# A decoder layer on one core: input sums of the seven-product scheme built by accumulating transfers from GpSimd

## The reference

```python
mod = silu(c) @ w_ada + b_ada                 # six shift/scale/gate vectors
h = rms_norm(x) * (1 + scale1) + shift1
proj = h @ w_in                               # columns for two head groups
# group A: 4 heads of gated linear attention; group B: 4 heads of HGRN2
x = x + gate1 * (concat(o_gla, o_hgrn) @ w_out)
h = rms_norm(x) * (1 + scale2) + shift2
x = x + gate2 * (square(relu(h @ w_mlp1)) @ w_mlp2)
return rms_norm(x, final_norm_g)
```

## Time and profile before

| | us |
|---|---|
| median of 3 runs | 1165.91 (1165.58 to 1169.56) |
| the profiled execution | 1166.44 |
| its span, first to last instruction | 1164.7 |
| PE busy in it | 1137.4 |
| DVE busy | 876.3 |
| ACT busy | 612.9 |
| POOL busy | 499.4 |

### The profile page before, as it was taken

How to read it: one execution, slowest core, us unless ns; L and a number is a source line. 1 busy time by engine, 2 the same in 40 slices (tenths; PEclk the granted TensorE clock), 3 DMA queues, 4 the chain that set the end, 5 groups by cost and what they waited for, 6 DMA issues and landing times.

```text
span 1164.7 us, 15675 instructions
## 1 busy us (share of the span) xinstructions
PE 1137.4 (98%) x5555; PEld 939.3 (81%) x5555; DVE 876.3 (75%) x1048; ACT 612.9 (53%) x933; POOL 499.4 (43%) x318
## 2 busy tenths in 40 slices
PE   7999999899999999999999999999999999999996
PEld 6788788787878787888888888888888888788885
DVE  6898888877777677477976765677795884966776
ACT  7763564756566566345654555455664433424424
POOL 1021111534243344427534353344466675666741
PEclk9999999999999999999999999999999999999999
DMA  9777353044353549421455344544624637447203
GB/s 359 259 235 271 128 175 97 1 127 129 93 177 98 154 123 295 143 93 73 137 170 181 136 155 135 181 144 157 194 64 159 223 91 264 147 132 279 72 1 145
DMA packets 160549, 180.44 MB, mean 155 GB/s; under 512 B 7508, under 2 KB 119256, under 8 KB 157784
## 3 DMA queue, kind: packets, MB, share of 16 engines
q1 hardware_dynamic: 160472, 179.44, 46.4%
HBM read 138.51 MB, written 40.89 MB: 154 GB/s over the span
## 4 chain that ended last, share of the span: by engine, by line
PE 89%; DVE 4%; DMA 2%; ACT 2%; issue 1%; SPq 1%; POOL 1%; DVEq 0%; ACTq 0%
PE unit_bank L1742 16%; PE unit_bank L2156 9%; PE unit_bank L2158 9%; PE unit_bank L2157 9%; PE small_bank L2156 9%; PE small_bank L2158 9%; PE small_bank L2157 9%; PE unit_bank L2003 3%; PE small_bank L1742 3%; PE unit_bank L2005 3%; PE unit_bank L2004 3%; PE small_bank L1879 2%; DVE ada_acc L2257 1%; PE small_bank L1781 1%; DMA ada_slot<-in_w_ada_dram 1%
## 5 line engine op out<-in xcount | busy, mean ns | idle before, releaser
L997 POOL TENSOR_TENSOR wr_lo<-quarter,wr_hi 128x512 fp32r<-128x512 f32 x122 | 197.6, 1632 | 174.4 <-ACT wr_hi L1530 174.3
L2156 PE MATMUL unit_bank<-op_hi,wr_hi 128*128 128x512 f32 x452 | 176.5, 390 | 1.1 <-issue 1.1
L2158 PE MATMUL unit_bank<-op_hi,wr_lo 128*128 128x512 f32 x452 | 175.9, 389 | 0.0
L2157 PE MATMUL unit_bank<-op_lo,wr_hi 128*128 128x512 f32 x452 | 175.9, 389 | 0.0
L2156 PE MATMUL small_bank<-op_hi,wr_hi 128*128 128x512 f32 x448 | 174.5, 390 | 0.0
L2158 PE MATMUL small_bank<-op_hi,wr_lo 128*128 128x512 f32 x448 | 174.3, 389 | 0.0
L2157 PE MATMUL small_bank<-op_lo,wr_hi 128*128 128x512 f32 x448 | 174.3, 389 | 0.0
L1530 ACT ACTIVATE wr_hi<-wr_full 128x512 fp32r<-128x512 f32 x90 | 56.8, 631 | 173.3 <-DVE wr_full L2903 173.3
L2903 DVE TENSOR_TENSOR wr_full<-quarter,quarter 128x512 f32<-128x512 f32 x90 | 88.9, 989 | 56.3 <-PE small_bank L2158 23.0
L1530 ACT ACTIVATE wr_hi<-quarter 128x512 fp32r<-128x512 f32 x136 | 83.0, 626 | 90.5 <-PE unit_bank L2158 48.4
L1742 PE MATMUL unit_bank<-a_hi,w_hi 128*128 128x512 f32 x304 | 121.2, 399 | 0.8 <-DVE w_lo L2401 0.8
(11 more groups left out here) (366 smaller groups left out, 2397.2 us busy)
## 6 DMA issues: line engine op xcount, KB each, us to landing
quarter<-in_w_mlp_dram SPq DMA_DIRECT2D x128, 256.0 KB, 4.1
hidden_scratch<-hid SPq DMA_DIRECT2D x98, 256.0 KB, 2.4
ada_slot<-in_w_ada_dram SPq DMA_DIRECT2D x48, 512.0 KB, 6.1
op_full<-hidden_scratch SPq DMA_DIRECT2D x21, 1024.0 KB, 4.8
pair_quarter<-in_w_in_dram SPq DMA_DIRECT2D x32, 256.0 KB, 3.7
piece_x<-t_scratch SPq DMA_DIRECT2D x16, 512.0 KB, 4.1
piece_y<-t_scratch SPq DMA_DIRECT2D x32, 256.0 KB, 3.3
raw<-in_w_out_dram SPq DMA_DIRECT2D x16, 512.0 KB, 4.5
```

The lines of the kernel that those rows point to most:

```text
L997: pool.tensor_tensor(wr_lo[slot][:, :, :], split_source(n), wr_hi[slot][:, :, :].bitcast(F32), ALU.subtract).then_inc(wr_lo_pool, 1)
L2156: pe.matmul(dst, wh, ah, start=opens, stop=False, skip_group_check=True)
L2157: pe.matmul(dst, wh, al, start=False, stop=False, skip_group_check=True)
L2158: mm = pe.matmul(dst, wl, ah, start=False, stop=k == KH - 1, skip_group_check=True)
```

## The change

The eight sums on DVE are gone. In their place POOL issues transfers from SBUF to SBUF of 1024 KB each: `carry_over` copies, `add_part` adds its source to what stands at its target (`accum_op=ALU.add`). Since a transfer can add and not subtract, the scheme's signs are turned: operands are now sums only, and the minus signs are in three places where DVE works anyway, without more operations: two weight sums change sign or operation, the third becomes a `scalar_tensor_tensor` of the same size, and two of the joins subtract. The order of the sums changes too: the third operand is `xs[3]` = q(0,1) + q(1,1), made by a copy and three adding transfers; `xs[1]`, a copy of it after the first two, receives q(0,0) beside it by two more.

POOL has 13 such transfers. Each waits for the landing of what it reads and adds to, and POOL's own operations stand behind those waits.

```diff
@@ gpsimd
+            def carry_over(dst, src, done):
+                pool.dma_start(dst[:, :, :], src).then_inc(done, 16)
+            def add_part(dst, part, k, half, done):
+                pool.dma_start(dst[:, :, :], blocks(part, k, half).bitcast(F32), accum_op=ALU.add).then_inc(done, 16)
+            def third_sum_begun():
+                pool.wait_ge(x_out, X_OUT_0 + 16 * KT)
+                pool.wait_ge(split_hi, 16)
+                pool.wait_ge(lo_dve, 16)
+                carry_over(xs[3], blocks(a_hi, 0, 1).bitcast(F32), first_sum)
+                pool.wait_ge(first_sum, 16)
+                add_part(xs[3], a_lo, 0, 1, first_sum)
+                pool.wait_ge(first_sum, 32)
+                carry_over(xs[1], xs[3][:, :, :], other_sum)
+            def two_sums(part, n):
+                pool.wait_ge(other_sum, 16 * n)
+                pool.wait_ge(first_sum, 16 * (n + 1))
+                add_part(xs[3], part, 1, 1, first_sum)
+                add_part(xs[1], part, 0, 0, other_sum)
+            def second_sum_begun():
+                pool.wait_ge(t3_stored, T3_STORED_0 + 32)
+                pool.wait_ge(other_sum, 48)
+                carry_over(xs[2], xs[1][:, :, :], other_sum)
+                pool.wait_ge(other_sum, 64)
+                add_part(xs[2], a_hi, 1, 1, other_sum)
+                pool.wait_ge(other_sum, 80)
+                add_part(xs[2], a_lo, 1, 1, other_sum)
+            def fourth_sum_part(part, n):
+                pool.wait_ge(first_sum, 16 * n)
+                add_part(xs[3], part, 1, 0, first_sum)
             for u in range(2, U_OUT):
                 low(u, u % 2)
+                if u == 7:
+                    third_sum_begun()
+                if u in (8, 9):
+                    two_sums((a_hi, a_lo)[u - 8], u - 7)
+                if u == 11:
+                    second_sum_begun()
+                if u == 12:
+                    pool.wait_ge(other_sum, 96)
+                    carry_over(xs[3], xs[2][:, :, :], first_sum)
+                    fourth_sum_part(a_hi, 5)
+            fourth_sum_part(a_lo, 6)
             pool.wait_ge(t_high, T_HIGH_0 + 2)
@@ scalar
-                    act.wait_ge(t_made, T_MADE_0 + 7)
+                    act.wait_ge(other_sum, 48)
                     act.activation(t1_hi[:, :, :], xs[1][:, :, :], ACT.Copy).then_inc(t_high, 1)
                     act.wait_ge(unit_filled[1], 13)
-                    act.activation(blocks(a_hi, 0, 1), xs[3][:, :, :], ACT.Copy).then_inc(t_high, 1)
+                    act.wait_ge(other_sum, 96)
+                    act.activation(blocks(a_hi, 0, 1), xs[2][:, :, :], ACT.Copy).then_inc(t_high, 1)
...
-                        act.wait_ge(t_made, T_MADE_0 + 3)
+                        act.wait_ge(first_sum, 64)
                         act.activation(t3_hi[:, :, :], xs[3][:, :, :], ACT.Copy).then_inc(t_high, 1)
...
-                    act.wait_ge(t_made, T_MADE_0 + 9)
-                    act.activation(t4_hi[:, :, :], xs[2][:, :, :], ACT.Copy).then_inc(t_high, 1)
+                    act.wait_ge(first_sum, 112)
+                    act.activation(t4_hi[:, :, :], xs[3][:, :, :], ACT.Copy).then_inc(t_high, 1)
@@ vector
-                if name == "P1":
-                    dve.wait_ge(x_out, X_OUT_0 + 16 * KT)
-                    add_parts(xs[1], 0, 1, 0)
-                    add_parts(xs[0], 1, 1, 1)
-                if name == "H0":
-                    dve.wait_ge(t3_stored, T3_STORED_0 + 32)
-                    add_parts(xs[2], 0, 0, 4)
-                    subtract(xs[1], xs[1], xs[2], 5)
                 read_out(3)
-                if name == "H0":
-                    subtract(xs[3], xs[0], xs[1], 6)
...
-                    subtract(xs[3], xs[0], xs[1], 2)
...
-                    add_parts(xs[2], 1, 0, 7)
-                    subtract(xs[2], xs[2], xs[3], 8)
...
-                    dst, a, b, op = pq[0], pq[3], pw_full[PAIR_PLACE[P7]], ALU.subtract
+                    dve.scalar_tensor_tensor(pq[0][:, :, :], pw_full[PAIR_PLACE[P7]][:, :, :], -1.0, pq[3][:, :, :],
+                                             ALU.mult, ALU.subtract).then_inc(pair_sum, 1)
...
-                dve.tensor_tensor(dst, a, b, ALU.add).then_inc(joined, 1)
+                dve.tensor_tensor(dst, a, b, ALU.subtract if c in ("22", "12") else ALU.add).then_inc(joined, 1)
```

More of the change, by code:

```diff
@@ L363, in hybrid_layer @@
         pw_full = {kb: at(f"pw_full{kb}", kb + 2, [P, KH, P]) for kb in (168, 172, 176, 180)}
-        xs = [at(f"x_sum{i}", 8 * i, [P, KH, HALF]) for i in range(4)]
+        xs = {i: at(f"x_sum{i}", 8 * i, [P, KH, HALF]) for i in range(1, 4)}
         t1_hi, t1_lo = at("t1_hi", 0, [P, KH, HALF], F32R), at("t1_lo", 8, [P, KH, HALF], F32R)
         t3_hi, t3_lo = at("t3_hi", 16, [P, KH, HALF], F32R), at("t3_lo", 24, [P, KH, HALF], F32R)
-        t4_hi, t4_lo = at("t4_hi", 24, [P, KH, HALF], F32R), at("t4_lo", 16, [P, KH, HALF], F32R)
+        t4_hi, t4_lo = at("t4_hi", 16, [P, KH, HALF], F32R), at("t4_lo", 24, [P, KH, HALF], F32R)
         piece_x = {kb: at(f"piece_x{kb}", kb, [P, 2, HALF], F32R) for kb in (120, 96)}
@@ L445, in hybrid_layer @@
         acc_added = sem("acc_added")
-        y_sum = sem("y_sum")
+        first_sum, other_sum = sem("first_sum"), sem("other_sum")
         stored = sem("stored")
@@ L2402, in low_out @@
                                   ).then_inc(wlo_out, 1)
-            def add_parts(dst, k, half, n):
-                if n:
-                    dve.wait_ge(t_made, T_MADE_0 + n)
-                dve.tensor_tensor(dst[:, :, :], blocks(a_hi, k, half).bitcast(F32), blocks(a_lo, k, half).bitcast(F32), ALU.add
-                                  ).then_inc(t_made, 1)
-            def subtract(dst, a, b, n):
-                dve.wait_ge(t_made, T_MADE_0 + n)
-                dve.tensor_tensor(dst[:, :, :], a[:, :, :], b[:, :, :], ALU.subtract).then_inc(t_made, 1)
             def low_third():
```

25 lines of the change are left out of this document (12 added, 13 removed).

## The result

The changed kernel takes **1190.1 us** (median of 4 runs, 1188.4 to 1192.5), the kernel before 1165.9 beside it on the same chip: a ratio of 1.0201, 95% interval 1.0172 to 1.0231. It is 24 us slower; the forecast was +9.5 and the range ended at 1190. Its profiled execution took 1192.5 us, the longest of the four, with a span of 1190.8 (before 1164.7), so the two traces stand 26.1 us apart.

The account below looks back on a forecast made before the run. PE was taken to bound the kernel, busy 1137.4 of 1164.7 us. The terms -0.5 + 7.5 + 2.5 gave +9.5 on the profiled execution's 1166.4, 1175.9, or 1175.4 us against the median; range 1163 to 1190.

Parts of the forecast that it names:

- the ceiling of the gain: First pair: all that DVE's sums cost PE, two waits for POOL and a lowered clock, 0.8 + 1.9 + 2.5 = 5.2 us.
- The term of -0.5: First pair: PE's waits for POOL go, ACT's `k_nat` is late next; between -3 and +0.8, taken as -0.5 us.
- The price of an add: One adding transfer of 1024 KB from SBUF to SBUF takes 7.2 us, bounds 4.8 and 9.6.
- two that are issued together take 12: A pair of adding transfers in the chains takes 2.4 + 4 x 2.4 = 12 us.
- The chain in P1: P1: serial transfers take 36.0 us from 119.8, plus 7.7 for SP's traffic, so `t3_hi` is 7.9 us late.
- The 15 us late: P1: by the skill's 6.15 us per 1 MB issued by GpSimd, `t3_hi` and PE would be late by some 15 us.
- PE's stall: Early in H0: PE waits for ACT's `vT`, 7.9 - 0.4 = 7.5 us.
- the price of the clock: Early in H0: the half clock after PE's wait for `vT` adds 2.5 us.
- The low part of unit 8: P1: POOL has it ready at 136.6 against PE's 142.19, so hidden with 5.6 us to spare.
- H0's chain: H0: transfers take 31.2 us from 179.2, POOL is free at 210.4, early enough by 4 us; cost zero.
- Rival 2: Adds at the upper bound of 9.6 us, `t3_hi` 17.5 us late; +20, about 1186 us; chance 0.12 with beyond.
- my likeliest case: The forecast itself, 1175.4 us, own range 1171 to 1182 for an add of 6.3 to 8.2 us; chance 0.42.

Follow-up runs that it names:

- k_nat_before_norm: `last_add_behind_t_lo` with ACT's `t4_hi` moved behind `k_nat`, and P6's high part and `k_nat` put ahead of the norm's exponentials; 0.9999 of the kernel before.
- last_add_behind_t_lo: Kernel before with only the fourth sum built by POOL's transfers, the last add issued behind the four `t_lo` subtractions; 1.001 of the kernel before.
- low_8_first: Changed kernel with POOL's low part of unit 8 taken between P1's first copy and first add; 1.0204 of the kernel before.

## Why the prediction was wrong

**What bounds, and the ceiling of the gain: right.** The 5.2 us at this place are real: `k_nat_before_norm` has the state updates 5.5 us earlier. They aren't a gain, since 4.3 of them are given back by 290 us.

**The term of -0.5: the mechanism right, the size near the bad end of its bounds.** `last_add_behind_t_lo` has POOL's subtractions at 1.3 us, the updates at 236.2 (I said 235.7), product P6 0.6 us earlier, and P5 0.8 us later (244.64 for 243.81, of which 0.3 stands from the start of that trace): my bound was +0.8, for 1.7 gained and 2.5 lost. It takes 1.2 us more in all. I had said "about 4 us of idling take the place of 2.7", and it was 4.1. The 231.5 us at which I had PE reach that point was a slip, since 231.98 - 2.7 + 2.8 is 232.1, and 232.1 is what the trace has.

**The price of an add: right, of a pair wrong.** 7.7 us undisturbed, to its landing, for the 7.2 taken, and bounds of 4.8 and 9.6 that held. But "two that are issued together take 12" was 13.6, and I counted the last step as a single add (7.2) although the change issues a pair there too: ACT waited 10.9 us for its half.

**The chain in P1: the mechanism right, its length wrong, and the step of the forecast that failed.** The term that failed is the 7.9 us by which `t3_hi` was to be late, and with it the 7.5 us at PE. I had 43.7 us from 119.8; it took 54.0 from 122.3. The 20.8 us are:

| term | predicted | measured |
|---|---|---|
| start behind `x_scratch` (from when POOL may issue) | 119.8 | 122.3, +2.5 |
| copy, add, copy, undisturbed | 16.8 | 17.1, +0.3 |
| the pair undisturbed, and the last step as it ran | 19.2 | 13.6 + 10.9, +5.3 |
| SP's traffic | 7.7 | 3.2 + 5.7 + 2.5 = 11.4, +3.7 |
| gaps between landing and next issue | 0 | about 1.1, +1.1 |
| late for ACT's want at 155.59 | 7.9 | 20.8 |

For the traffic I take what each step took above its undisturbed size: the copy 7.9 for 4.7, the add 13.4 for 7.7, the pair 16.1 for 13.6. That this is traffic is what is left over, not measured by itself; the 13.6, from issue to issue, holds some 0.3 us of the gaps. The last step had 1.4 MB of SP's beside it, so part of its 10.9 us is traffic too. The start was in my rows: the earlier trace rows has DVE's first sum at 121.7, behind the same wait, where I read the end of SP's traffic off a stretch; 0.9 us of the lateness is that execution's own, ahead of the chain. Each term was off in the same direction, and all are serial, so they add up without anything to hide them. By the Trainium skill, "Collectives: The Full Stack", section "Why ReduceScatter is half of AllGather", an adding step runs at half a copy's rate: here 201 against 426 GB/s for the same rows of 2 KB, so the trace agrees. By the Trainium skill, "DMA: Bandwidth & Descriptors", section "Measured (HBM→SBUF, 128 partitions, SWDGE, issued from GpSimd)", 1 MB takes 6.15 us; the figure is for another way than from SBUF to SBUF, where it is 4.5 to 4.7 from issue to landing undisturbed. The 15 us late that I drew from it were nearer to the 20.8, but by a term that isn't there.

**PE's stall: the transfer of the lateness right, the price of the clock too high.** 20.8 late at ACT became 20.5 at PE, with the clock at 0.50 in the wait and 0.84 in the 3 us behind it. For that clock I had 2.5 us; it was 1.5, from 20.5 at the turning of `vT` to 22.0 at the matmul at 190.24 (168.23 before). The low part of unit 8, "hidden, with 5.6 to spare", made PE wait 4.2 us; it cost nothing that can be measured, as `low_8_first` shows.

**H0's chain, "cost zero": wrong.** POOL's last issue stood 37.5 us behind the chain's start, where I had 31.2: 2.6 more for the adds and 3.7 for the copies, one of them beside SP's traffic. I then asked only when POOL would be free for its own work. What cost was what POOL's work, now directly behind an issue, did to DVE: in the changed kernel 3.5 us of PE's waiting for `mod`, and 2.8 us less are lost there with the line moved. Rival 2 was the nearest case (+20, slow adds), with 0.12; its size was right for another reason, since the adds weren't at their upper bound. That is luck, as is the end of the range at 1190. And the top of my likeliest case, 1182, doesn't follow from its add of 8.2 us: by the same sum that is 4 us more than 1175.4, or 1179.4.

**The sum.** I had 7.5 + 2.5 - 0.5. In the two traces it is 19.6 (20.5 without the 0.9 that stood ahead of the chain), 1.5 and 3.6.

**What the profile after would show.** ACT's wait of over 5 us, PE's for `vT` with the clock behind it, and POOL's 1.3 us came as written. The clock fell again too, but behind the state updates and not ahead of them: 1.00 in 257.5 to 261 us, in which PE waits 2.5 us for `k_nat`, then 0.63 in 262 to 266. PE waited for a low part of weights too, one of my signs of being wrong, but that wasn't the cost.
